# Hybrid HGRN2 / sparse-attention trunk: a gate column or output product between a tile's key transposes and its state update

## The reference, cut to what matters

```python
proj = xn @ w_in[layer]     # all columns of HGRN2, attention, indexer and gates
y_a = hgrn2_mixer(hq, hf, hi, hg, ...)   # S = diag(f) S + (1-f) outer i;  o = S^T q;  rmsnorm per head;  o * silu(hg)
y_b = dsa_mixer(aq, ak, av, iq, ik, iw, ...)   # scores of the chosen keys, softmax, product with v
merged = sigmoid(gate_a) * (y_a @ w_branch_hgrn) + sigmoid(gate_b) * (y_b @ w_branch_dsa)
h = h + merged @ w_out[layer]
h = h + hier_moe(rmsnorm(h), ...)        # 32 experts, top 2
```

## Time and profile before

| | busy us | share of the span |
|---|---|---|
| TensorE matmul | 1486.8 | 84% |
| TensorE weight load | 1159.5 | 66% |
| VectorE | 708.0 | 40% |
| ScalarE | 584.1 | 33% |
| GpSimd | 343.1 | 19% |

### The profile page before, as it was taken

How to read it: one execution, slowest core, us unless ns; L and a number is a source line. 1 busy time by engine, 2 the same in 40 slices (tenths; PEclk the granted TensorE clock), 3 DMA queues, 4 the chain that set the end, 5 groups by cost and what they waited for, 6 DMA issues and landing times.

```text
span 1760.8 us, 30301 instructions
## 1 busy us (share of the span) xinstructions
PE 1486.8 (84%) x11834; PEld 1159.5 (66%) x11834; DVE 708.0 (40%) x1718; ACT 584.1 (33%) x1047; POOL 343.1 (19%) x235
## 2 busy tenths in 40 slices
PE   3999976979999599988579999589899986998882
PEld 3879966977777455554268799588768674555551
DVE  5137987034352411111243399830454324111114
ACT  5234554255422011111243445433554220111112
POOL 4201341220300022222032024113003001222210
PEclk8999986989999599999879899679899986999996
DMA  6111230112253799999632113102024366999994
GB/s 227 49 49 68 83 140 14 61 49 79 84 192 135 281 372 384 387 393 391 242 140 97 49 49 127 68 20 97 18 73 138 133 263 258 383 384 393 393 378 170
DMA packets 91990, 321.95 MB, mean 183 GB/s; under 512 B 15376, under 2 KB 15760, under 8 KB 75232
## 3 DMA queue, kind: packets, MB, share of 16 engines
q1 hardware_dynamic: 75376, 289.46, 43.7%
q0 software_dynamic: 10240, 17.33, 3.0%
q10 hardware_dynamic: 6256, 13.51, 2.1%
HBM read 302.49 MB, written 34.01 MB: 191 GB/s over the span
## 4 chain that ended last, share of the span: by engine, by line
PE 53%; SPq 17%; DVE 15%; issue 6%; DMA 4%; ACT 4%; POOL 0%; ACTq 0%; DVEq 0%; POOLq 0%
PE ps L740 14%; PE ps L763 12%; SPq L558 10%; SPq L564 6%; PE ps L1034 5%; PE ps L750 3%; PE ps L975 3%; DMA r<-w_expert_up 2%; PE ps L1055 2%; DVE sc L1368 2%; PE ps L955 2%; PE ps L983 1%; PE ps L731 1%; PE ps L928 1%; PE ps L1023 1%
## 5 line engine op out<-in xcount | busy, mean ns | idle before, releaser
L763 PE MATMUL ps<-x_high,chunk_high_a 128*128 128x264 f32 x896 | 269.5, 301 | 10.7 <-POOL gate_up_low L2099 7.2
L763 PE MATMUL ps<-x_high,gate_up_low 128*128 128x264 f32 x896 | 265.7, 297 | 0.0
L763 PE MATMUL ps<-x_low,chunk_high_a 128*128 128x264 f32 x896 | 265.7, 297 | 0.0
L2099 POOL TENSOR_TENSOR gate_up_low<-gu_ring,chunk_high_a 128x1024 fp32r<-128x1024 f32 x56 | 135.0, 2423 | 478.3 <-ACT chunk_high_a L1742 478.3
L763 PEld LDWEIGHTS ps<-x_high,chunk_high_a 128*128 128x128 f32 x896 | 180.6, 202 | 14.8 <-issue 14.3
L763 PEld LDWEIGHTS ps<-x_low,chunk_high_a 128*128 128x128 f32 x896 | 180.5, 201 | 0.0
L763 PEld LDWEIGHTS ps<-x_high,gate_up_low 128*128 128x128 f32 x896 | 180.3, 201 | 0.0
L1648 DVE COPY r<-ps 128x512 f32<-128x512 f32 x64 | 44.3, 692 | 303.0 <-PE ps L1023 303.0
L2150 POOL DMA_INDIRECT r<-xrow,idx x64 | 61.4, 960 | 490.8 <-PE ps L1023 260.8
L740 PE MATMUL ps<-gate_up_low,x_high 128*128 128x512 f32 (+1 forms) x352 | 140.5, 399 | 0.0
L2025 ACT ACTIVATE r<-ps 128x256 f32<-128x256 f32 x64 | 24.6, 384 | 314.0 <-PE ps L1034 314.0
(11 more groups left out here) (337 smaller groups left out, 3009.2 us busy)
## 6 DMA issues: line engine op xcount, KB each, us to landing
gu_ring<-w_in SPq DMA_DIRECT2D x20, 2048.0 KB, 9.2
r<-w_expert_down SPq DMA_DIRECT2D x44, 512.0 KB, 19.4
gu_ring<-w_expert_gate SPq DMA_DIRECT2D x20, 1024.0 KB, 19.4
gu_ring<-w_expert_up SPq DMA_DIRECT2D x20, 1024.0 KB, 25.4
dn_ring<-w_expert_down SPq DMA_DIRECT2D x40, 512.0 KB, 18.7
expert<-w_expert_gate SPq DMA_DIRECT2D x12, 1024.0 KB, 17.7
expert<-w_expert_up SPq DMA_DIRECT2D x12, 1024.0 KB, 23.4
expert<-w_expert_down SPq DMA_DIRECT2D x24, 512.0 KB, 19.4
```

Of the source, the lines that this page charges most:

```text
L763: last = mm(o[:, lo:hi], w[:, c, quarter(name, j)], x[:, c, lo:hi], start=c == 0 and k == 0, stop=c == KC - 1 and k == 2)
L2099: G.tensor_tensor(low[:, :, cols], w[:, :, cols], high[:, :, cols].bitcast(F32), ALU.subtract).then_inc(sem["low_p"], 1)
```

## The change

- Between the key transposes of a tile and its state update TensorE now does another job: gate 10 and 11 for tiles 0 and 1, output products 0 and 1 for tiles 2 and 3.
- VectorE waits for ("su", j) and then, for j above 1, for ("ot", j-1), each by name.
- The scores of heads 0 to 3 move from behind "on" to ahead of the last output-gate column; ScalarE takes their four Exp there, between the Silu of columns 2 and 3.
- The scores of heads 4 to 7 move behind gate 12.
- VectorE takes the maxima 0 to 3, the divisions 0 to 3, then maxima 4 and 5, and goes on as before; `hgrn_output` comes after m = 4, 7, 10, 13.
- ScalarE takes gate 12 out of its slab before the Exp of heads 4 to 7, not after it.

```diff
     for j in range(NT - 1):
-        add(("kt", j), ("su", j))
-        if j < 2:
-            add(GATES[10 + j])
-        if 0 < j < NT - 2:
-            add(("ot", j - 1))
+        add(("kt", j), GATES[10 + j] if j < 2 else ("ot", j - 2), ("su", j))
     for j in range(HH):
         if j > 0:
             add(("ot", j + 1))
+        if j == HH - 1:
+            add(*[("qk", 0, h) for h in range(4)])
         add(("hg", j))
     add(*[("on", h) for h in range(HH)])
-    add(*[("qk", 0, h) for h in range(4)])
     for n, (i, g) in enumerate(groups):
-        if n == 0:
-            add(*[("qk", 0, 4 + r) for r in range(4)])
-        elif AHEAD <= n < len(groups) - 1:
+        if AHEAD <= n < len(groups) - 1:
             ...
         add(FILL[n])
+        if n == 0:
+            add(*[("qk", 0, 4 + r) for r in range(4)])
...
                 for j in range(NT - 1):
-                    done(("ot", j - 1) if j > 1 else ("su", j))
+                    done(("su", j))
+                    if j > 1:
+                        done(("ot", j - 1))
...
-                score_max(0)
-                score_max(1)
-                for m in range(40):
+                for m in range(4):
+                    score_max(m)
+                for m in range(4):
+                    normalise(m)
+                score_max(4)
+                score_max(5)
+                for m in range(4, 40):
                     if m + 2 < 40:
                         score_max(m + 2)
                     normalise(m)
-                    if m % 4 == 1 and m < 16:
-                        hgrn_output(m // 4)
+                    if m in (4, 7, 10, 13):
+                        hgrn_output((m - 4) // 3)
...
                 gate_out(11)
+                state_rows(2)
                 output_rows(0)
-                state_rows(2)
+                state_rows(3)
                 output_rows(1)
-                state_rows(3)
                 for j in range(HH):
                     if j > 0:
                         output_rows(j + 1)
+                    if j == HH - 1:
+                        for m in range(4):
+                            softmax_exp(m)
                     done(("hg", j))
...
-                for m in range(4):
-                    softmax_exp(m)
                 for n0 in range(2 * NT):
+                    if n0 == 0:
+                        gate_out(SLOT3)
                     if n0 + 1 < 2 * NT:
                         for m in range(4 * n0 + 4, 4 * n0 + 8):
                             softmax_exp(m)
-                    if n0 < 4:
+                    if 0 < n0 < 4:
                         gate_out(SLOT3 + n0)
```

More of the change, by code:

```diff
@@ L861, in _, with key_rows_out @@
                 freed(("lv", HP - 1, LEVELS - 1))
-                def update(j):
+                def key_rows_out(j):
                     n = TS[j]
@@ L869, in update @@
                     last.then_inc(sem["pe_done"], 1)
+                def update(j):
+                    n = TS[j]
                     s = take(("su", j))
@@ L891, in output, with scores @@
                     last.then_inc(sem["pe_done"], 1)
+                def scores(i, g):
+                    for hd in range(4 * g, 4 * g + 4):
+                        take(("qk", i, hd))
+                        if TS[i] <= 64:
+                            settle(pe)
+                        o = wide(("qk", i, hd))
+                        r = 64 * (hd % 2)
+                        for lo, hi in spans(W[i]):
+                            last = mm(o[0:TS[i], lo:hi], aqk[r:r + 64, hd // 2, T0[i]:T0[i] + TS[i]],
+                                      aqk[r:r + 64, 4 + g, lo:hi], start=True, stop=True, tile_position=(r, 0))
+                        last.then_inc(sem["pe_done"], 1)
                 for j in range(NT - 1):
-                    update(j)
+                    key_rows_out(j)
                     if j < 2:
                         gate(10 + j)
-                    if 0 < j < NT - 2:
-                        output(j - 1)
+                    else:
+                        output(j - 2)
+                    update(j)
                 for j in range(HH):
@@ L901, in _ @@
                         output(j + 1)
+                    if j == HH - 1:
+                        scores(0, 0)
                     project("hg", "hg", j, 1, j)
@@ L918, in fill @@
                     feature_major(("wa", c), lambda k: w[:, k, c * P:(c + 1) * P], lambda k, lo, hi: hq[:, k, lo:hi], HH)
[L920 to L932, removed]
                 groups = [(i, g) for i in range(NT) for g in range(2)]
@@ L935, in _ @@
                 for n_, (i, g) in enumerate(groups):
-                    if n_ == 0 or AHEAD <= n_ < len(groups) - 1:
+                    if AHEAD <= n_ < len(groups) - 1:
                         scores(*groups[n_ + 1])
                     fill(n_)
+                    if n_ == 0:
+                        scores(*groups[1])
                     n = TS[i]
@@ L1928, in _, with softmax_exp @@
                 gate_out(11)
+                state_rows(2)
                 output_rows(0)
-                state_rows(2)
+                state_rows(3)
                 output_rows(1)
-                state_rows(3)
+                def softmax_exp(m):
+                    i, hd = m // 8, m % 8
+                    n = TS[i]
+                    act.wait_ge(*at("mx_ready", m + 1))
+                    A(pb[0:n, hd, 0:W[i]], pb[0:n, hd, 0:W[i]], ACT.Exp, bias=nmx[0:n, hd:hd + 1], scale=AD ** -0.5,
+                      accum_out=psum_[0:n, hd:hd + 1]).then_inc(sem["p_ready"], 1)
                 for j in range(HH):
```

## The result

The changed kernel took 1747.2 us, the median of 4 runs (1743.6 to 1751.9), against 1760.8 for the kernel before, now the median of 4 runs (the first three had 1759.31): a ratio of 0.9922, 95% interval 0.9899 to 0.9945. It is faster, by 13.6 us and not by the 26 that were forecast, and 1.2 us above the stated range. Its profiled execution has a span of 1750.3 us; the one before had 1760.8, by chance the same figure as the median.

A forecast was written before the change was run, and what follows sets the result against it. TensorE's waits were taken as the bound, each costing itself and the 1.2 GHz clock behind it. Layers gain 7.0 + 3.5 = 10.5 and 11.7 + 3.75 = 15.45, together 26 us: median 1733 us, 8 in 10 range 1725 to 1746.

The forecast's parts named there:

- Part 1: Update stage, first transposes to first output-gate column: copies hidden, 0.45 us new VectorE wait, 20.7 us stage.
- a gain of 7.0 and 11.7 us: Update stage saving in first and second layer, from 27.69 and 32.38 us down to 20.7.
- Part 2: Scores of heads 0 to 3 ahead of last output-gate column: it starts 1.05 us later per layer, maxima and divisions hidden.
- Part 3: "On" jobs to gate 13: 17.1 us instead of 22.6 and 22.85; net gain 3.5 and 3.75 us after deductions.
- 0.35 at gate 14: Loss at gate 14, with `hgrn_output` after m = 10 ahead of the maximum freeing its slab: 0.35 us.
- 3.5 to 3.75 of the forecast: Net gain per layer from scores, gate 12 and softmax order: 3.5 us in the first layer, 3.75 in the second.
- The low clock: Rival: gates 10 and 11 fall to the 1.2 GHz level, gate 12 stays low; 11.4 us lost, time 1744; chance 0.18.
- The tail: Rival: stretch behind gate 12 no longer than before; 2 x 4.35 us more gained, time 1724; chance 0.06.
- the softmax lag: Rival: 7.2 us lag behind gate 12 returns at following groups, 4.35 us each; 1768 with four; chance 0.05.
- no weight chunk is late: Against the no-change rival: late weight chunk or memory row eats either stage's gain; time 1757; chance 0.05.

The follow-up runs named there:

- eight readings: Update stage in the old order, by layer: kernel before profiled twice, plus two other kernels leaving that stage as it was; 26.18 to 32.38 us, mean 29.07.
- the whole change: The changed kernel with all its edits, timed three times against the kernel before: ratios 0.9922, 0.9902, 0.9896.
- third_early: Changed kernel with the third HGRN output after division 9 instead of 10; ratio 0.9882 to the kernel before.
- filled pauses: Kernel before with two to four extra 128x256 constant matmuls between a tile's transposes and its update; ratio 0.9982.

## Why the prediction was wrong, point by point

- **Part 1, the mechanism: right.** The copies are hidden, the new wait for VectorE is 0.42 us (0.45), the stage 20.92 us in every execution.
- **Part 1, the size: wrong.** The step that failed is "a gain of 7.0 and 11.7 us". The subtrahend was right; 27.69 and 32.38 were one execution's clock. The mean of eight readings is 29.07, so the gain is 16.3 us and not 18.7. The rivals looked for low clock after the change and none for an unusually low one before it.
- **Part 2: right.** The output-gate stage went from 28.82 to 30.01 us, 1.2 later (1.05); the table loads and Exp are hidden.
- **Part 3 up to gate 13: right.** 3.86 + 6.11 + 7.56 = 17.53 us (17.1). VectorE stands at the first division until the Exp of head 4, then takes the HGRN output, as counted.
- **Part 3, gate 14: wrong, and the larger miss.** "0.35 at gate 14, where `hgrn_output` after m = 10 now stands ahead of the maximum" names the cause and prices the wait alone. The pause grew by 0.63 us; with it came, in five of the six layers of the whole change, a lower clock in gates 14 and 15, in the two later stretches or in both. From the first "hg" column to the router (without the gap between gate 15 and the branch columns, which is equal), the six layers of the whole change take 0.5 us more than before in the mean (215.5 against 215.0). third_early's two layers take 3.3 less (211.7), close to the 3.5 to 3.75 of the forecast. That is about 4 us per layer, 8 in all by the traces; by the times the move of that output is worth 2.5 to 7 us.
- Together: 26 - 2.4 - 8 = 15.6, against 13.6 in the first timing and some 16 over all three. The 8 is an estimate from eight layers; by the times it would be less, and some us would stay open.
- **Rivals.** The low clock (the first rival, which the part on transposes calls the second) stood at 1744 and came near in time by luck, for the wrong place: gates 10 to 12 are at 1.00 in every trace of the change. What came was low clock at gates that this rival did not list. The tail is as long as counted, the softmax lag does not come back at later groups, and no weight chunk is late.
- What the Trainium skill says of transposes ("TensorE: Matmul & The Clock Gate", Part 4), that the full rate does not engage for them, did not show: the stage with all its transposes has a PEclk of 1.00 in every trace of the new order, and in the filled pauses. Of the switch of tables that the Trainium skill prices ("ScalarE: Activation LUTs", What ACT_TABLE_LOAD costs) as a load and a drain, again only the load shows: behind gate 12 the Sigmoid starts 1.29 us after its load.

What stays open: why 0.63 us of pause more moves the clock of stretches that begin up to 90 us later. The runs show that the loss goes with it in ten layers of 14, and that the course differs between layers and executions (8.6 and 8.4, or 7.4 and 63.3, or no loss). They don't show what in it the clock answers to.

## What to carry to other kernels

A stall on TensorE has two prices, itself and the clock behind it; so has a stall of half a microsecond that a reordering leaves somewhere else, and it may be paid in stretches nobody touched. For every wait that a change lengthens, ask what the matmuls behind it would take at the lower clock, and not only how long it is. Before a low clock is booked as a gain, look at a second execution of the same kernel: here one stage had 26.2 to 32.4 us with no edit to it, and 27.7 to 32.4 in one kernel.

## What the runs showed of the hardware that was not expected

- The same instructions had a granted clock of 0.79, 0.88, 0.94 or 1.00 in different layers and executions (update stage in the old order: 32.38, 29.23, 27.69, 26.18 us), while gates 14 and 15 of the kernel before were at 7.6 and 6.1 us in all four layers of its two profiles. Some places are steady and others not.
- A pause of 3.47 us of sparse work instead of 2.84 ahead of one gate column went with 2.6 to 5.6 us more behind it in ten layers of 14, and the shorter pause in none of 14; in some layers much of that is in stretches that begin 30 and 90 us later (63.34 and 74.29 us at 0.97 and 0.98, against 61.64 and 72.77 at 1.00).
- TensorE with matmuls of no use in its pauses (26.18 us at 1.00 in both layers of one execution) was faster in that stage than TensorE waiting there (29.07 in the mean of eight readings).
